# The last pair of tiles of a two-layer trunk: a quarter of the expert picks taken out of the gathers and computed densely from 32 blocks

## The reference, cut to what matters

```
q = (h @ w_query).reshape(T, 8, 256)
v1, i1 = top_k(q[..., :128] . sub_keys[0], 16)     # 16 of 128 rows of keys
v2, i2 = top_k(q[..., 128:] . sub_keys[1], 16)
sc, ci = top_k(v1[:, None] + v2[None, :], 16)      # 16 of the 256 sums
e = i1[ci // 16] * 128 + i2[ci % 16]               # one of 16384 experts
gate = softmax(sc)
x += sum over 8 heads and 16 picks of  gelu(expert_u[e] . h) * gate * expert_v[e]
```

## Time and profile before

| | us |
|---|---|
| median of 3 runs | 2942.43 (2940.84 to 2944.15) |
| span of the profiled execution | 2935.5 |
| median less the span: what lies around it | 6.9 |
| slot 512's dot product begins (from here pass 4 runs) | 1573.4 |
| slot 588's | 1792.7 |
| slot 649's | 1950.1 |
| slot 768's (the last pair's first) | 2273.4 |
| slot 1023's (the last) | 2918.7 |

### The profile page before, as it was taken

One profiled execution on the slowest core, in us unless ns is written; L12 is line 12 of the kernel. 1 busy time (PEld: TensorE's weight loads), 2 busy tenths in 40 slices (PEclk: granted clock), 3 DMA queues, 4 the chain that ended last, 5 costly groups with the idle time before them and its releaser, 6 DMA issues.

```text
span 2935.5 us, 37444 instructions
## 1 busy us (share of the span) xinstructions
PE 2322.3 (79%) x12254; PEld 921.1 (31%) x12254; DVE 2030.7 (69%) x4798; ACT 1344.2 (46%) x3701; POOL 1281.8 (44%) x1063
## 2 busy tenths in 40 slices
PE   8889877888967987788976898888886676666665
PEld 7634344343512342242421343333341111111110
DVE  2778867886388657886458767787547777777544
ACT  2333634954344338734334435853444444444433
POOL 0334444444435434444335434454434555555553
PEclk9999788999968997888977998888996666666666
DMA  9799999999999999999999999999999999999997
GB/s 361 288 358 403 403 404 419 420 420 419 412 419 416 412 418 414 420 403 420 416 416 409 414 412 421 408 404 420 420 420 421 411 421 421 421 406 421 421 421 292
DMA packets 202346, 1192.22 MB, mean 406 GB/s; under 512 B 25384, under 2 KB 38184, under 8 KB 68520
## 3 DMA queue, kind: packets, MB, share of 16 engines
q0 software_dynamic: 147456, 1073.81, 88.6%
q1 hardware_dynamic: 54696, 116.03, 10.5%
HBM read 1187.67 MB, written 2.10 MB: 405 GB/s over the span
## 4 chain that ended last, share of the span: by engine, by line
DMA 44%; PE 28%; DVE 9%; ACT 9%; issue 6%; POOL 3%; SPq 0%; POOLq 0%; DVEq 0%; ACTq 0%
DMA arena<-in_uv,eidx 41%; PE acc L1896 11%; PE bank L1574 7%; DVE arena L1558 5%; PE bank L1822 4%; PE bank L1656 3%; POOL arena L848 3%; DMA unit<-in_w_in 2%; ACT L1090 2%; ACT L982 1%; ACT wts L1094 1%; ACT gelu L1090 1%; DMA unit<-in_w_query 1%; ACT diag L1102 1%; PE heads L1574 1%
## 5 line engine op out<-in xcount | busy, mean ns | idle before, releaser
L848 POOL DMA_INDIRECT arena<-in_uv,eidx x1024 | 1246.2, 1217 | 1455.1 <-PE acc L1896 1175.9
L1896 PE MATMUL acc<-arena,diag 64*64 64x512 f32 x7888 | 1370.5, 780 | 544.3 <-ACT diag L1102 514.4
L1558 DVE CUSTOM_DVE_ANT_0 arena<-arena,h 128x1024 f32<-128x1024 f32 x1024 | 1254.1, 1226 | 733.1 <-DMA arena<-in_uv,eidx 727.4
L1090 ACT ACTIVATE gelu<-dots,stat 128x1 f32<-128x1 f32 x1024 | 299.9, 293 | 1305.9 <-DVE dots L1558 1302.5
L1896 PEld LDWEIGHTS acc<-arena,diag 64*64 64x64 f32 x7888 | 246.9, 157 | 1349.9 <-ACT diag L1102 1185.5
L1102 ACT ACTIVATE diag<-identc,wts 128x64 f32<-128x64 f32 x986 | 343.0, 348 | 32.3
L1094 ACT ACTIVATE wts<-gelu,gate 128x1 f32<-128x1 f32 x1024 | 301.6, 295 | 33.4
L1822 PE MATMUL bank<-h,unit 128*128 128x256 f32 (+1 forms) x1024 | 230.4, 372 | 8.4 <-DMA unit<-in_w_query 8.4
L1822 PEld LDWEIGHTS bank<-h,unit 128*128 128x128 f32 x1024 | 171.8, 197 | 116.8 <-issue 91.8
L1574 PE MATMUL bank<-unit,h 128*128 128x512 f32 (+1 forms) x336 | 137.6, 541 | 0.0
L1656 PE MATMUL bank<-h,unit 128*128 128x256 f32 (+2 forms) x480 | 123.3, 404 | 0.0
(11 more groups left out here) (218 smaller groups left out, 1753.1 us busy)
## 6 DMA issues: line engine op xcount, KB each, us to landing
unit<-in_w_in SPq DMA_DIRECT2D x36, 1024.0 KB, 20.9
unit<-in_w_query SPq DMA_DIRECT2D x35, 1024.0 KB, 12.4
arena<-in_uv,eidx POOLq DMA_INDIRECT x1024, 17.2
unit<-in_w_out SPq DMA_DIRECT2D x16, 1024.0 KB, 9.7
arena<-in_w_in SPq DMA_DIRECT2D x8, 1024.0 KB, 9.5
arena<-in_w_query SPq DMA_DIRECT2D x5, 1024.0 KB, 19.6
arena<-in_w_out SPq DMA_DIRECT2D x4, 1024.0 KB, 14.3
x<-in_x SPq DMA_DIRECT2D x4, 512.0 KB, 10.1
```

Source lines behind the costliest of these rows:

```text
L848: nc.gpsimd.indirect_dma_start(arena[:, n % NBUF, :], None, uv, bass.IndirectOffsetOnAxis(ap=eidx[:, seq % 2, j:j + 1], axis=0)).then_inc( ...
L1090: nc.scalar.activation(gelu[:, group], dots[:, group], ACT.Gelu_apprx_tanh, scale=r2[:, seq:seq + 1]).then_inc(s_ge, GROUP)
L1558: V.tensor_tensor_reduce(out=uu, in0=uu, in1=h_nat[seq % 3], scale=1.0, scalar=0.0, op0=ALU.mult, op1=ALU.add, accum_out=dots[:, n % BODY: ...
L1896: ins = nc.tensor.matmul(acc[rows][cols * HALF:(cols + 1) * HALF, :], diag[own, n % NBUF, :], arena[own, n % NBUF, D + f * 512:D + (f + 1) ...
```

## The change

It concerns the last pair of tiles (layer 1, tiles 2 and 3: slots 768 to 1023, `Q0` = 6 is their first tile in the order of slots). A pick whose block i1 is below 32 gets an expert number 65536 too high; the gathers get a bounds check, by which such rows are left out, and their gate in the slots is zero. The gathers stay 256. Beside the slots, the 32 blocks are read once (32 loads of u and 32 of v, 512 KB each, on SP's queue into the ring that held weights) and made densely for all 256 positions:

- the gates are brought into the form [expert in block, block, position]: for each position, VectorE makes one-hot rows of i2 and of i1 times gate, TensorE multiplies them (a 128 by 128 by 32 matmul a position), 16 groups of 16 positions, ScalarE copies out;
- for each block TensorE turns u (8 transposes, ScalarE copies), multiplies it with h (8 matmuls of 256 columns), ScalarE takes gelu, VectorE multiplies with the gates, TensorE multiplies with v (4 matmuls of 512 columns) and accumulates in the 4 PSUM banks of the passes.

For the working memory of this, pass 4 must be over: `pace(4)` becomes slots 512 to 588 in place of 512 to 748. The routing of the chunks before (r 17 to 23, the last three of tile 0 and the four of tile 1) is moved to 9 slots each from slot 512, 3 parts a slot; that of the last pair (r 24 to 31) to 7 slots each from slot 592, 4 parts a slot. `BESIDE` is then slot 649, and `pair_due` spreads the dense steps over slots 649 to 1008, on all engines at the same n: by the weights some 4.4 slots for a group (slots 652 to 722) and 7.9 slots for a block (slots 722 to 975). From slot 649 on every third slot (8 to 111 of each 128) is summed by VectorE instead of TensorE. The tiles for this share memory with the passes' tiles; the last h has a place of its own. In the dense steps the dot products of the slots go to two scratch rows.

The diff's core; after the constants and plan follow SP, GpSimd, ScalarE, VectorE and TensorE. In the step of a block e each engine does what stands in its `for e in range(JT + 1)`.

```
+MIX_SLOTS = 76
+PICK_LATE, PICK_PAIR = (9, 3), (7, 4)
+EIGHT = 8
+PART = 32
+BLOCKS = 32
...
+    PD = NP - 1
+    Q0 = first_seq[PD]
+    NT = len(passes[PD][1]) * P
+    JT = BLOCKS
     NSLOTS = first_slot(NP)
+    CHUNK_ALL = first_seq[NP] * CHUNKS
...
+        if p == PD:
+            return first_slot(p - 1), first_slot(p - 1) + MIX_SLOTS
...
+        if n >= BESIDE:
+            return n % 3 == 2 and 8 <= n % SLOTS < SLOTS - 16
...
+        if seq >= Q0:
+            return pace(PD)[1] + 4 + PICK_PAIR[0] * (r - Q0 * CHUNKS), PICK_PAIR[1]
+        if first_seq[PD - 1] * CHUNKS < r:
+            return first_slot(PD - 1) + PICK_LATE[0] * (r - first_seq[PD - 1] * CHUNKS - 1), PICK_LATE[1]
...
+    BESIDE = route_at(CHUNK_ALL - 1)[0] + -(-route_parts(CHUNK_ALL - 1) // PICK_PAIR[1]) + 1
+
+    GT = 2 * EIGHT
+    GROUPS = NT // GT
+
+    pair_weights = [10, 10, 20] + [50] * GROUPS + [90] * JT + [40, 10] + [20] * 8 * len(runs[0][:2])
+    pair_sums = list(accumulate(pair_weights))
+
+    def pair_due(n):
+
+        a, b = BESIDE, NSLOTS - 16
+        n -= n % SLOTS < ADD_AT
+        if n < a:
+            return 0
+        return sum(v * (b - a) <= pair_sums[-1] * min(n + 1 - a, b - a) for v in pair_sums)
...
+            last_l = passes[PD][0]
+            for j in range(JT):
+                rows = slice(last_l * NE + j * P, last_l * NE + (j + 1) * P)
+                if j == 0:
+                    wait_unit_used(sp, *last_in_ring(0))
+                elif j >= U_PLACES:
+                    sp.wait_ge(s_tr, 2 * (j - U_PLACES + 1))
+                sp.dma_start(u_place[j % U_PLACES], uv[rows, 0:D]).then_inc(s_ul[j % U_PLACES], 16)
+                if j in (0, 2):
+                    wait_unit_used(sp, *last_in_ring(1 + j // 2))
+                elif j >= V_PLACES:
+                    sp.wait_ge(s_v, j - V_PLACES + 1)
+                sp.dma_start(v_place[j % V_PLACES], uv[rows, D:2 * D]).then_inc(s_vl[j % V_PLACES], 16)
+            sp.wait_ge(s_au, JT)
...
+            def pair_experts(p):
+                yield from idle(3 + GROUPS + JT + 2)
...
+                    bass.IndirectOffsetOnAxis(ap=numbers(seq)[:, j:j + 1], axis=0),
+                    bounds_check=L * NE - 1, oob_is_err=False).then_inc(s_land[n % NBUF], 16)
...
+                def keys_turned(e, half):
+                    if e == 0:
+                        act.wait_ge(s_h, 2 * first_seq[NP])
+                    act.wait_ge(s_tr, 2 * e + half + 1)
+                    nc.scalar.activation(uT[:, half * 512:(half + 1) * 512], heads[1][:], ACT.Copy).then_inc(s_tc, 1)
+
+                def gate_columns(g):
+                    act.wait_ge(s_gm, 2 * g + 2)
+                    nc.scalar.activation(g_all[:, :, g * GT:(g + 1) * GT], heads[0][:].rearrange("p (t j) -> p j t", t=GT),
+                                         ACT.Copy).then_inc(s_gc, 1)
+
+                for half in range(2):
+                    keys_turned(0, half)
+                yield 1
+                for g in range(GROUPS):
+                    gate_columns(g)
+                    yield 1
+                for e in range(JT + 1):
+                    if e + 1 < JT:
+                        keys_turned(e + 1, 0)
+                    if e < JT:
+                        act.wait_ge(s_au, e + 1)
+                        if e >= ACTS:
+                            act.wait_ge(s_v, e - ACTS + 1)
+                        nc.scalar.activation(e_act[:, e % ACTS, :], heads[0][:, 0:NT], ACT.Gelu_apprx_tanh).then_inc(s_ag, 1)
+                    if e + 1 < JT:
+                        keys_turned(e + 1, 1)
+                    yield 1
...
+                    step(V.tensor_scalar(epart[:, 1, k], i1, float(BLOCKS), None, ALU.is_ge))
+                    step(V.scalar_tensor_tensor(out=epart[:, 0, k], in0=i1, scalar=float(KEYS), in1=i2, op0=ALU.mult, op1=ALU.add))
+                    step(V.tensor_scalar(epart[:, 0, k], epart[:, 0, k], float(l * NE) + FAR, None, ALU.add))
+                    step(V.scalar_tensor_tensor(out=epart[:, 0, k], in0=epart[:, 1, k], scalar=-FAR, in1=epart[:, 0, k],
+                                                op0=ALU.mult, op1=ALU.add))
+                    V.tensor_copy(far_idx[:, seq - Q0, c * CS + lo * K:c * CS + hi * K], epart[:, 0, k]).then_inc(s_idx, n)
+                    dve.wait_ge(s_idx, HC * chunk_no(seq, c) + hi)
+                    return
...
+                def one_hots(g):
+                    t = g * GT
+                    if g == 0:
+                        dve.wait_ge(s_iota, 1)
+                    dve.wait_ge(s_pc, t // P + 1)
+                    for half in range(2):
+                        k = 2 * g + half
+                        own = slice(t % P + half * EIGHT, t % P + (half + 1) * EIGHT)
+                        i1, i2, weight = [picked[:, t // P, a, own].unsqueeze(2) for a in range(3)]
+                        if k >= 2:
+                            dve.wait_ge(s_gm, k - 1)
+                        V.tensor_tensor(hot[half], iota_all.unsqueeze(1).broadcast_to([P, EIGHT, P]),
+                                        i2.broadcast_to([P, EIGHT, P]), ALU.is_equal)
+                        step(V.tensor_tensor(hot_j[half], iota_all[:, 0:PART].unsqueeze(1)
+                                             .broadcast_to([P, EIGHT, PART]), i1.broadcast_to([P, EIGHT, PART]), ALU.is_equal))
+                        V.tensor_tensor(hot_j[half], hot_j[half], weight.broadcast_to([P, EIGHT, PART]),
+                                        ALU.mult).then_inc(s_hot, 1)
+
+                for g in range(GROUPS):
+                    one_hots(g)
+                    yield 1
+                for e in range(JT + 1):
+                    if e < JT:
+                        if e == 0:
+                            dve.wait_ge(s_gc, GROUPS)
+                        dve.wait_ge(s_ag, e + 1)
+                        V.tensor_tensor(e_act[:, e % ACTS, :], e_act[:, e % ACTS, :], g_all[:, e, :],
+                                        ALU.mult).then_inc(s_w, 1)
+                    yield 1
+                dve.wait_ge(s_v, JT)
...
+                def turn_keys(e, half):
+                    pe.wait_ge(s_pc, 1)
+                    if half == 0:
+                        pe.wait_ge(s_ul[e % U_PLACES], 16 * (e // U_PLACES + 1))
+                    if e or half:
+                        pe.wait_ge(s_tc, 2 * e + half)
+                    for c in range(4):
+                        col = (4 * half + c) * P
+                        ins = nc.tensor.transpose(heads[1][:, c * P:(c + 1) * P], u_place[e % U_PLACES][:, col:col + P], ident[:])
+                    ins.then_inc(s_tr, 1)
+
+                def dot_keys(e, half):
+                    pe.wait_ge(s_tc, 2 * e + half + 1)
+                    if half == 0:
+                        pe.wait_ge(s_gc, GROUPS)
+                        if e:
+                            pe.wait_ge(s_ag, e)
+                    for c in range(4 * half, 4 * half + 4):
+                        ins = mm(heads[0][:, 0:NT], uT[:, c * P:(c + 1) * P], hT[:, c, 0:NT], c == 0, c == DC - 1)
+                    if half:
+                        ins.then_inc(s_au, 1)
+
+                def gate_columns(g):
+                    if g:
+                        pe.wait_ge(s_gc, g)
+                    else:
+                        pe.wait_ge(s_pc, 2)
+                    for half in range(2):
+                        pe.wait_ge(s_hot, 2 * g + half + 1)
+                        for k in range(EIGHT):
+                            at = (half * EIGHT + k) * PART
+                            ins = mm(heads[0][:, at:at + PART], hot[half][:, k, :], hot_j[half][:, k, :], True, True)
+                        ins.then_inc(s_gm, 1)
+
+                def sum_values(e):
+                    pe.wait_ge(s_vl[e % V_PLACES], 16 * (e // V_PLACES + 1))
+                    pe.wait_ge(s_w, e + 1)
+                    for i in range(NT // P):
+                        for f in range(2):
+                            ins = nc.tensor.matmul(banks[2 * i + f][:], e_act[:, e % ACTS, i * P:(i + 1) * P],
+                                                   v_place[e % V_PLACES][:, f * 512:(f + 1) * 512],
+                                                   start=e == 0, stop=e == JT - 1, skip_group_check=True)
+                    ins.then_inc(s_v, 1)
...
+                for e in range(JT + 1):
+                    for half in range(2):
+                        if e < JT:
+                            dot_keys(e, half)
+                        if e + 1 < JT:
+                            turn_keys(e + 1, half)
+                    if e:
+                        sum_values(e - 1)
+                    yield 1
...
+                advance(pair, pair_due(n) - paired[0], paired)
+            advance(pair, 10 ** 6, paired)
```

(23 more changed lines are left out.)

204 lines of the change are left out of this document (157 added, 47 removed).

## The result

The changed kernel takes 3140.6 us (median of 4, 3138.0 to 3145.0) against 2943.3 us before on the same chip: 1.0674 times as long, 95% interval 1.0660 to 1.0687. Forecast was 3190 us, with a range of 3060 to 3320. The profiled execution took 3140.56 us with a span of 3138.7: only 1.9 us lie around a span, not the 6.9 that the prediction took.

What follows compares the result with a forecast made beforehand. The prediction took the transfer stream as the bound before, with packed engine work slowing the change: 1573.4 us before slot 512, B 375, C 230, D 332, E 658, end 17, span 3185, forecast 3190 us, range 3060 to 3320.

Steps and rivals of the forecast that it cites:

- B: Slots 512 to 588, holding all of pass 4: 219 us before, 375 forecast, bounds 336 and 425, set by PE.
- C: Slots 588 to 649, eight chunks of packed routing: 157 us before, 230 forecast, bounds 215 and 250, set by DVE.
- D: Slots 649 to 768, one-hot groups and first blocks: 323 us before, 332 forecast, between 321 and 370.
- E: Slots 768 to 1023, rows left out beside block steps: 645 us before, 658 forecast, bounds 543 and 820.
- the floor of the transfers: In E, a slot's gather with rows left out needs 1.83 us of transfers, 2.15 with a block every 7.9 slots.
- The likeliest case: The forecast itself, chance 0.55, 3110 to 3270 us: in E, block steps making three engines wait eat the saving.
- the 169 us: Transfer time of the last pair's gathers said to go, 26.5% of picks left out; block loads add 80 us.
- The signs: What the later profile should show: times, PE and DVE shares and GB/s by stretch, gelu waits, bytes moved by queue.
- The step hides: Rival, chance 0.2: the block steps' waits in E cost nothing, E goes by transfers at 543 us, total 3077.
- rows not saved: Rival, chance 0.1: queues move something for each row left out; D unchanged, E 702 us, total 3236.
- GpSimd: Rival, chance 0.1: gather issues wait for two VectorE instructions each; E costs 3.2 us a slot, 819, total 3353.
- PE packs the pass: Rival, chance 0.05: pass 4's matmuls shrink, B falls to its transfers, 247 us, block step hidden, total 2923.

Runs made afterwards that it cites:

- The schedule alone: Changed kernel with its packed pass 4 and routing, nothing left out of the gathers and no dense part, against the kernel before: 1.0648.
- run 3: Not a follow-up run: in "run 3 slots late" the word is a verb, said of the pass's last steps on ScalarE and VectorE.

## Why the prediction was right

- **The change would be slower, by 8.4%.** It is, by 6.7%, for the reason given: pass 4's and the routing's work no longer fits beside the slots into which it was moved. The schedule alone gives 1.0648.
- **B, 375 us.** 345 to slot 588, but 374 to slot 592: the pass's last steps run 3 slots late on ScalarE and VectorE. The forecast for B and C together was 605 us, and it is 600; that the one was 30 too long and the other 25 too short is where the boundary fell. The floor was 336 to 344 us of PE work, and PE is busy for 342, of which the pass's are 243 and not 254. The 30 us for waits in program order were a guess that held (374 - 342 = 32). How little gives way when PE's work does was not foreseen: 34 sums taken from it gave 10 us back.
- **C, 230 us.** 226 us for slots 592 to 649 and 29 for the four before, which the prediction had in B. VectorE's 94% there, and the 143 us that these slots took with the routing spread, show that VectorE's routing set the time.
- **D, 332 us.** 311. Forecast were 2.75 us for a slot with one-hots; slots 652 to 722 took 176.5 us, 2.52 a slot, so ScalarE's wait was set too high. Without the dense part D takes 292 us, so groups and first blocks cost 19.
- **E, 658 us.** 631, with errors that partly cancel: slots 768 to 975 took 518 us and not 562, the rest 113 and not 96. A block on PE was forecast at 10 us. The rows of after, PE in slots 768 to 975 (26 blocks):

```profile
L1801 PE MATMUL heads<-h,gain 128*128 128x256 f32 x416 | 108.0, 405 | 0.0
L2155 PE MATMUL bank<-unit,acts 128*128 128x512 f32 x208 | 93.6, 593 | 0.0
L2124 PE MATMUL heads<-ident,unit 128*128 128x128 f32 x208 | 31.4, 274 | 0.0
```

  give 108.0 / 26 = 4.2 for the dots, 1.2 for the turns and 3.6 for the values, 9.0 in all, and VectorE's loss was 6 to 7 us a block and not 8 to 9, at a clock of 0.86 and not 0.8. That made E shorter. On the other side the floor of the transfers, 1.83 us a slot, was never reached: the packets' length is right, but without any dense part a slot took 2.03. That the queues would keep running without gaps once the bytes fell was assumed without a row for it. The likeliest case named VectorE's wait as what eats the saving; when it was taken away 20 of E's 631 us went, so this is the part of the mechanism that was mostly wrong. What eats the saving is more even. Of the 169 us, 125 came (645 to 520 without the dense part). The dense part takes 111 back: its loads take 11.6% of 631 us, or 73, and the other 38 no run divides further than the 20 that the multiply's place gave.
- **The signs.** B, its transfers and PE's share came as named (345 us, 285 GB/s, 91%); the gathers' bytes fell by 71 MB and SP's rose by 34. C took 255 us and not some 230, with VectorE at 94% only from slot 592 on. Slots 768 to 975 took 2.50 us each, under the 2.6 to 2.8, at 356 GB/s.
- **Rivals.** "The step hides" gave 543 for E, "rows not saved" 702 (the run that gathers them has 707.5, so its working was right for another kernel), "GpSimd" 819. None came. For the last, GpSimd stood 105 us for VectorE's adds in slots 768 to 975, but by way of the free place in `arena`; its issues in E took 1.34 us on the mean, 1.38 before. "PE packs the pass" needed 0.51 us for 256 columns to shrink. In the packed pass, slots 512 to 592, they did a little:

```profile
L2049 PE MATMUL bank<-h,unit 128*128 128x256 f32 x256 | 61.0, 392 | 1.2 <-ACT h L987 1.2
```

  61.0 / 128 = 0.48 us, where the same group had 65.2 / 128 = 0.51. The whole pass became 11 us shorter; the rival needed B at 266 us.

Still open is how B's 32 us of waits divide, and what leaves the gaps in the queues once rows are left out: GpSimd's issues, the nine places, or both. No run had fewer than 32 blocks, so whether a smaller dense part would pay is not tested.

## What to carry to other kernels

A saving in the resource that bounds a kernel has to be charged with what must be moved to make room for it: here 118 us of gathers were bought with 190 us of work packed into stretches where TensorE or VectorE then needed longer than the transfers. Work out, for each stretch and each engine, the whole of its work over the slots it is given; it took three rows here, and no version paid such a stretch back elsewhere. Where a step is dealt out at the same slot on engines that wait for one another, put the consumer's part one step later first: it gave 26 and 41 us for moving one multiply. And a share of busy queues is not a rate: read it beside the GB/s, and before a byte is called dearer look at a stretch with the same share and nothing left out.

## What the runs showed of the hardware

An indirect DMA with rows out of bounds keeps a packet of 4 bytes for each (36.4 to 36.6 thousand packets for E's gathers, with the rows and without; 12.7 thousand of them under 512 B where rows are left out, 4.1 thousand where not). The packets that stay keep their length, 309 ns at the median, 312 before. Where the queues aren't kept full, some packets take far longer (over 450 ns: 11% in slots 592 to 649 of the changed kernel, 0.4% in E of before), so the DMA share overstates what is moved: 0.97 went with 379 GB/s, 1.00 with 413. A bounds check costs nothing when all rows are in (1.0003), though an issue's median goes from 0.95 to 1.00 us. And TensorE's mean granted clock was 0.81 and not 0.88 in slots 512 to 592 when 34 slot sums were taken from it there.
